# Strassen's scheme for two pairs of feed-forward chunks, and the norm's factors moved from weights to activations

## What is computed

```python
def swiglu(h, w_gate, w_up, w_down):
    return (jax.nn.silu(h @ w_gate) * (h @ w_up)) @ w_down

for l in range(2):
    x = x + 0.5 * swiglu(rms_norm(x, ffn1_norm[l]), ffn1_w_gate[l], ffn1_w_up[l], ffn1_w_down[l])
    ...                                  # attention and pooling, "mix" below
    x = x + 0.5 * swiglu(rms_norm(x, ffn2_norm[l]), ffn2_w_gate[l], ffn2_w_up[l], ffn2_w_down[l])
return rms_norm(x, final_norm)
```

## Time and profile before

| | before |
|---|---|
| median of 3 runs | 936.33 us (936.30 to 936.41) |
| profiled execution | 936.85 us, its span 934.7 us |
| TensorE busy | 925.4 us, 99% |
| VectorE busy | 551.5 us, 59% |
| ScalarE busy | 502.0 us, 54% |
| GpSimd busy | 44.5 us, 5% |
| moved by DMA | 174.67 MB, mean 187 GB/s |

### The profile page before, as it was taken

How to read it: one execution, slowest core, us unless ns; L and a number is a source line. 1 busy time by engine, 2 the same in 40 slices (tenths; PEclk the granted TensorE clock), 3 DMA queues, 4 the chain that set the end, 5 groups by cost and what they waited for, 6 DMA issues and landing times.

```text
span 934.7 us, 12762 instructions
## 1 busy us (share of the span) xinstructions
PE 925.4 (99%) x4313; PEld 759.4 (81%) x4313; DVE 551.5 (59%) x896; ACT 502.0 (54%) x825; POOL 44.5 (5%) x84
## 2 busy tenths in 40 slices
PE   8999999999999999999999999999999999999997
PEld 6788888887778888888888888888877888888886
DVE  5655465559756655556476455564787564554644
ACT  6554454557637545545365455453675464554543
POOL 0010100010001001001010000000100000000000
PEclk9999999999999999999999999999999999999999
DMA  7867778855245677786465657646434276465441
GB/s 245 293 157 209 212 169 235 291 201 185 91 136 178 194 221 198 179 240 168 128 227 197 208 190 250 205 158 214 135 141 147 74 261 206 162 212 192 158 157 45
DMA packets 123676, 174.67 MB, mean 187 GB/s; under 512 B 8400, under 2 KB 99712, under 8 KB 123392
## 3 DMA queue, kind: packets, MB, share of 16 engines
q1 hardware_dynamic: 117744, 165.43, 52.8%
q0 software_dynamic: 2848, 6.38, 5.8%
q10 hardware_dynamic: 3056, 2.49, 0.8%
HBM read 173.14 MB, written 4.19 MB: 190 GB/s over the span
## 4 chain that ended last, share of the span: by engine, by line
PE 96%; DMA 1%; DVE 1%; SPq 1%; ACT 0%; issue 0%; POOLq 0%; POOL 0%
PE ps L1036 29%; PE ps L1039 29%; PE ps L1037 29%; PE ps L1133 2%; DMA w_raw<-in_ffn_w_up_dram 1%; PE ps L1095 1%; PE ps L1046 1%; PE ps L1047 1%; PE ps L1117 1%; PE ps L1271 1%; PE ps L1287 1%; PE ps L1299 1%; PE ps L1315 1%; SPq L313 0%; DVE w_lo L778 0%; PE ps L1259 0%
## 5 line engine op out<-in xcount | busy, mean ns | idle before, releaser
L1036 PE MATMUL ps<-w_hi,xt_hi 128*128 128x512 f32 x848 | 337.5, 398 | 1.1 <-DVE xt_lo L792 0.7
L778 DVE SCALAR_TENSOR_TENSOR w_lo<-w_raw,gains,w_hi 128x512 fp32r<-128x512 f32 x416 | 285.0, 746 | 86.1 <-ACT w_hi L508 82.4
L1037 PE MATMUL ps<-w_lo,xt_hi 128*128 128x512 f32 x848 | 330.5, 390 | 0.0
L1039 PE MATMUL ps<-w_hi,xt_lo 128*128 128x512 f32 x848 | 325.9, 390 | 0.0
L508 ACT ACTIVATE w_hi<-w_raw,gains 128x512 fp32r<-128x512 f32 x408 | 260.8, 714 | 77.6 <-PE ps L1039 76.6
L767 DVE TENSOR_TENSOR w_lo<-w_raw,w_hi 128x1024 fp32r<-128x1024 f32 x104 | 122.7, 1221 | 124.0 <-ACT w_hi L501 123.7
L1036 PEld LDWEIGHTS ps<-w_hi,xt_hi 128*128 128x128 f32 x848 | 159.3, 188 | 36.0 <-issue 2.8
L1039 PEld LDWEIGHTS ps<-w_hi,xt_lo 128*128 128x128 f32 x848 | 159.2, 188 | 34.0
L1037 PEld LDWEIGHTS ps<-w_lo,xt_hi 128*128 128x128 f32 x848 | 159.5, 188 | 30.7
L501 ACT ACTIVATE w_hi<-w_raw 128x1024 fp32r<-128x1024 f32 x104 | 104.4, 1052 | 116.2 <-PE ps L1039 116.2
L1036 PE MATMUL ps<-w_hi,gt_hi 128*128 128x512 f32 (+1 forms) x356 | 138.7, 390 | 0.0
(11 more groups left out here) (95 smaller groups left out, 423.4 us busy)
## 6 DMA issues: line engine op xcount, KB each, us to landing
w_raw<-in_ffn_w_down_dram SPq DMA_DIRECT2D x88, 512.0 KB, 4.3
w_raw<-in_ffn_w_gate_dram SPq DMA_DIRECT2D x86, 512.0 KB, 4.0
w_raw<-in_ffn_w_up_dram SPq DMA_DIRECT2D x86, 512.0 KB, 5.2
w_raw<-in_w_in_dram SPq DMA_DIRECT2D x32, 512.0 KB, 4.9
w_raw<-in_w_out_dram SPq DMA_DIRECT2D x16, 512.0 KB, 5.4
bias_scratch<-in_rpb_dram POOLq DMA_DIRECT2D x32, 96.0 KB, 6.1
bias<-bias_scratch POOLq DMA_DIRECT2D x2, 1536.0 KB, 7.7
resid<-in_x_dram SPq DMA_DIRECT2D x4, 256.0 KB, 5.0
```

Of the source, the lines that this page charges most:

```text
L778: nc.vector.scalar_tensor_tensor(w_lo[slot][:, part], w_raw[slot][:, part], g, w_hi[slot][:, part].bitcast(F32), ALU.mult, ALU.subtract).t ...
L1036: nc.tensor.matmul(o, hi, wh, start=start, stop=False)
L1037: nc.tensor.matmul(o, hi, wl, start=False, stop=False)
L1039: last = nc.tensor.matmul(o, lo, wh, start=False, stop=bool(stop))
```

## The change

**Pairs.** A stage's 11 chunks are now: chunks 0 and 1 as before, then twice a body of four chunks (`ff_body`, index j; i = 4j + 2), then chunk 10. In a body chunks i and i + 3 are ordinary, and chunks i + 1 and i + 2 (3+4 and 7+8) are a pair. Its gate and up product is a 2 x 2 block product: A is the activation (rows: the two tiles, columns: the two halves of the width), B the weights (rows: halves of the width, columns: the two chunks). Seven block products with sums of A's and of B's blocks take the place of eight (the variant of Strassen's scheme with operands A11, A12, A22, S1 to S4), each of 12 matrix instructions (`seventh`). They go into banks 7 (X), 0 (Z) and 1 (Y).

**Sums.** B's four sums are made by VectorE in place in the raw units (`add_units`, 2048 columns), the seven combinations of the results also by VectorE (`combine`, into `normed`'s four quarters `p1`, `m5`, `u`, `c11`), two copies of results out of PSUM by ScalarE. A's sums S1 to S4 are made once a stage.

**Slots.** Two more slots E and F hold units of the pairs. They and the new operands' low parts lie where the mix's `scores`, `z`, `bias`, `pool_m` and `final_gain` lie, so `pool_m` is loaded in each layer and `final_gain` in the last stage.

**Factors.** From chunk 2 on the weights are split without the norm's factors. The activation is multiplied instead: once a stage GpSimd adds `xt_hi` and `xt_lo` into `normed` (two sums of 1024 columns), ScalarE multiplies by the factors in place (eight of 256 columns), ScalarE and VectorE split it into `xs_hi`, `xs_lo`, then GpSimd makes the four sums S in series (512 columns each), and both split these too.

GpSimd, new, between `rstd_of` and the gathers of each feed-forward stage:

```diff
+            def x_sums(layer, ff):
+                number = layer * STAGES + ff["stage"]
+                n = ff_no(layer, ff)
+                pool.wait_ge(xt_lo_ready, number * 4 + 4)
+                for t in range(TT):
+                    nc.gpsimd.tensor_tensor(
+                        normed[:, t, :],
+                        xt_hi[:, t, :, :].rearrange("p k q -> p (k q)").bitcast(F32),
+                        xt_lo[:, t, :, :].rearrange("p k q -> p (k q)").bitcast(F32), ALU.add
+                    ).then_inc(x_summed, 1)
...
+                pool.wait_ge(x_lo_ready, 4 * n + 2)
+                nc.gpsimd.tensor_tensor(block(1, 1), block(1, 1), block(1, 0), ALU.subtract
+                                        ).then_inc(s_summed, 1)
+                pool.wait_ge(s_summed, 4 * n + 1)
+                nc.gpsimd.tensor_tensor(block(1, 0), block(0, 0), block(1, 0), ALU.add
+                                        ).then_inc(s_summed, 1)
...
```

ScalarE, the stage (the first steps) and the body:

```diff
+                split_hi(d, d, raw_no(layer, stage, d, 0), (down_used, down_no(layer, ff, 1)))
+                scale_x(layer, ff)
+                store_gt_hi(layer, ff, 0)
+                x_hi(layer, ff)
+                silu_of(layer, ff, 1, 0)
+                split_hi(a, a, raw_no(layer, stage, a, 2), (g0_used, ord_no(layer, ff, 1) + 1))
+                silu_of(layer, ff, 1, 1)
+                split_hi(b, b, raw_no(layer, stage, b, 2))
+                s_hi(layer, ff)
+                with act.Fori(0, BODIES) as j:
+                    ff_body(layer, ff, j)
...
+                plain(d, d, 3 * j + 1, (down_used, down_no(layer, ff, i)))
+                plain(e, e, 2 * j, (g0_used, ord_no(layer, ff, 2 * j + 1) + 1))
+                store_gt_hi(layer, ff, i - 1)
+                silu_of(layer, ff, 2 * j + 2, 0)
+                sum_hi(f, e, 4 * n + 1, (gu_ready[1], ord_no(layer, ff, 2 * j + 1) + 1))
+                plain(a, a, 2 * j + 3, (g0_used, ord_no(layer, ff, 2 * j + 2) + 1))
+                silu_of(layer, ff, 2 * j + 2, 1)
+                plain(b, b, 3 * j + 3)
+                plain(d, d, 3 * j + 2, (down_used, down_no(layer, ff, i + 1)))
+                copy_m(BANK_X, 7 * n + 1, p1)
+                copy_m(BANK_Z, 7 * n + 2, m5)
+                sum_hi(e, b, 4 * n + 3, (m_ready, 7 * n + 1))
+                store_gt_hi(layer, ff, i)
+                sum_hi(f, f, 4 * n + 2, (m_ready, 7 * n + 2))
...
+                sum_hi(a, a, 4 * n + 4, (m_ready, 7 * n + 3))
...
+                plain(e, e, 2 * j + 1, (m_ready, 7 * n + 5))
...
+                plain(f, f, 2 * j + 1, (m_ready, 7 * n + 6))
...
+                store_gt_hi(layer, ff, i + 1)
+                plain(a, d, 3 * j + 3, (m_ready, 7 * n + 7))
...
```

VectorE, the body (`lo` is the low part of a unit, `gate_pair` a gate with both operands in SBUF; ahead of the loop the list is as ScalarE's, with `x_lo` behind `store_gt_lo(0)` and `s_lo` last):

```diff
+                lo(d, 3 * j + 1, d)
+                lo(e, 3 * j, e)
+                store_gt_lo(layer, ff, i - 1)
+                gate(layer, ff, 2 * j + 2, 0)
...
+                add_units(e, f)
+                lo(f, 3 * j, e)
+                lo(a, 4 * j + 3, a)
+                gate(layer, ff, 2 * j + 2, 1)
+                lo(b, 2 * j + 3, b)
...
+                add_units(f, b)
+                dve.wait_ge(sum_ready, 4 * n + 2)
+                add_units(b, e)
+                lo(d, 3 * j + 2, d)
+                lo(e, 3 * j + 1, b)
+                store_gt_lo(layer, ff, i)
...
+                combine(c11, ps[:, BANK_X, :], p1, ALU.add)
+                lo(f, 3 * j + 1, f)
+                gate_pair(c11, gated, 0, 0, 4 * n + 1)
...
+                add_units(a, b)
+                dve.wait_ge(m_ready, 7 * n + 5)
+                combine(u, ps[:, BANK_Y, :], p1, ALU.add)
...
+                combine(m5, m5, u, ALU.subtract)
...
+                combine(p1, ps[:, BANK_Z, :], m5, ALU.add)
+                lo(a, 4 * j + 4, a)
+                gate_pair(p1, gated_x, 0, 1, 4 * n + 2)
+                dve.wait_ge(m_ready, 7 * n + 6)
+                combine(u, ps[:, BANK_Y, :], u, ALU.add)
+                combine(m5, ps[:, BANK_Y, :], m5, ALU.subtract)
+                lo(e, 3 * j + 2, e)
...
+                combine(u, ps[:, BANK_X, :], u, ALU.subtract)
+                gate_pair(m5, gated_x, 1, 0, 4 * n + 3)
+                lo(f, 3 * j + 2, f)
+                gate_pair(u, gated, 1, 1, 4 * n + 4)
+                store_gt_lo(layer, ff, i + 1)
+                lo(a, 4 * j + 5, d)
+                lo(d, 3 * j + 3, b)
+                store_gt_lo(layer, ff, i + 2)
+                gate(layer, ff, 2 * j + 3, 0)
+                lo(a, 4 * j + 6, a)
+                lo(b, 2 * j + 4, b)
+                gate(layer, ff, 2 * j + 3, 1)
```

TensorE, the body:

```diff
+                ordinary(layer, ff, 2 * j + 2, 0, (a, b), units)
+                transpose_gated(layer, ff, 2 * j + 1)
+                ordinary(layer, ff, 2 * j + 2, 1, (a, b), units)
+                whole_down(layer, ff, i - 1, d, 3 * j + 1)
+                pe.wait_ge(x_lo_ready, 4 * ff_no(layer, ff) + 4)
+                seventh(layer, ff, BANK_X, e, 3 * j, A11)
+                pe.wait_ge(gated_ready[0], ord_no(layer, ff, 2 * j + 2) + 1)
+                seventh(layer, ff, BANK_Z, f, 3 * j, S1)
+                transpose_gated(layer, ff, 2 * j + 2)
+                pe.wait_ge(m_copied, 2 * n + 1)
+                seventh(layer, ff, BANK_X, a, 4 * j + 3, A12)
+                pe.wait_ge(m_copied, 2 * n + 2)
+                seventh(layer, ff, BANK_Z, b, 2 * j + 3, S4)
+                seventh(layer, ff, BANK_Y, e, 3 * j + 1, S2)
+                whole_down(layer, ff, i, d, 3 * j + 2)
+                pe.wait_ge(combined, 7 * n + 2)
+                seventh(layer, ff, BANK_Y, f, 3 * j + 1, S3)
+                pe.wait_ge(combined, 7 * n + 1)
+                seventh(layer, ff, BANK_X, a, 4 * j + 4, A22)
...
+                units = (3 * j + 2, 3 * j + 2)
+                pe.wait_ge(combined, 7 * n + 4)
+                ordinary(layer, ff, 2 * j + 3, 0, (e, f), units, {4: transpose_x})
+                whole_down(layer, ff, i + 1, a, 4 * j + 5)
+                pe.wait_ge(pair_gated, 4 * n + 4)
+                transpose_tiles(gated)
+                pe.wait_ge(combined, 7 * n + 6)
+                ordinary(layer, ff, 2 * j + 3, 1, (e, f), units)
+                whole_down(layer, ff, i + 2, d, 3 * j + 3)
```

SyncE loads in the order in which the units are used, from the body's E on only once the stage's first gate and up product is done. In the body it waits before each load until the raw unit's last reader is done; the end of a body goes as follows:

```diff
+                    free(d, 3 * j + 3)
+                    load_down(layer, weights, i + 1, d)
+                    sp.wait_ge(sum_ready, 4 * pair_no(layer, ff, j) + 4)
+                    load_down(layer, weights, i + 2, b)
+                    free(a, 4 * j + 5)
+                    load_gate_up(layer, weights, i + 4, 0, a)
+                    free(d, 3 * j + 4)
+                    load_gate_up(layer, weights, i + 4, 1, b)
```

467 lines of the change are left out of this document (336 added, 131 removed).

## The result

| | before | after |
|---|---|---|
| median of 4 runs each, same chip | 936.37 us | 950.84 us (950.47 to 952.86) |
| ratio, with its interval | 1 | 1.016 [1.0148, 1.0172] |
| span of the profiled execution | 934.7 us | 948.7 us |

The kernel became 1.6% slower. The forecast was 938.3 us, the range ended at 950.0, so the result lies outside it. The page after, to be held against the earlier trace rows: the span, the busy times, TensorE's granted clock in 40 slices, the chain by engine.

What follows compares the result with a forecast made beforehand. TensorE was taken as the bound, busy 925.4 of 934.7 us. From 936.85, minus 21.8 for products, plus 3 x 5.75 + 6.55 = 23.8 of waits, gave 938.85; the runs' median being 0.5 lower, 938.3 us, range 924 to 950.

Steps and rivals of the forecast that it cites:

- Products: TensorE's gate and up products: 84 in place of 96 per two chunks, 0.227 us each, 21.8 us less.
- The steady body: Four-chunk body with VectorE starting on time: TensorE needs 64.5 us and stalls 0.85 us a body.
- about 0.5 us at F and 0.3 at the a unit: TensorE's expected waits for w_lo in each body, for f's first half and for the a unit, eight times.
- VectorE late in every body: Slower rival: longer VectorE waits use up the 0.5 us slack in each of eight bodies; 945 to 955 us, chance 0.18.
- The start of a stage: GpSimd's new sums, in turns with w_lo, delay each stage's first body; 5.75 us lost a stage, 6.55 in the first.
- turn: GpSimd's new sums and VectorE's w_lo, both with two SBUF operands, alternate: 1.08 us a sum, 1.2 a w_lo half.
- L: VectorE's lateness in a stage's first body: 12.0 us after body start where 7.7 is steady, 4.3 us; first stage 3.1.
- +0.3: Predicted lengthening in us of each stage but the first: 5.45 us of products gained, 5.75 lost.
- The estimate of 1.2 and 2.3 us: GpSimd's sums of 512 and 1024 columns by the Trainium skill; would make the forecast sum about 941 us.
- At nothing: Items priced at zero, SP's new waits among them: units free 7 to 9 us early, transfers landing in 5.2.
- The rival with this mechanism: Transfers set the pace: five units asked for within some 10 us, about 5 us in each second body; 958 us, chance 0.06.

Runs made afterwards that it cites:

- c4: c3 with the two wide sums of 1024 columns also on VectorE, ahead of the first gate, so GpSimd makes no sum; 936.07 us.
- e1: Kernel after, with the 16 gathers of layer 1's attention bias moved from layer 0's second feed-forward stage to layer 0's mix; 948.74 us.
- e2: Kernel after, with the second body's E and F units asked for as soon as their slots are free; 940.48 us.
- e5: Kernel after without GpSimd's four serial sums S1 to S4, blocks of A standing in for them; 937.35 us.
- c3: Kernel after with three alterations: E and F asked for early, sums S on VectorE, order behind S3 altered; 933.50 us, again 934.54 us.

## Why the prediction was wrong, and where it was right

**Products: right.** 96 fewer, 0.227 us apart in the new blocks, at full clock.

**The steady body: right in place, with the terms swapped about.** The forecast had about 0.5 us at F and 0.3 at the a unit; the waits view has eight of 0.3 and eight of 0.2, the body 65.64 for 65.35. "VectorE late in every body", the rival of the slower side, did not happen.

**The start of a stage: right, with two sums mis-sized that nearly cancel, which is luck.** GpSimd's 512 columns take 1.30 us and not 1.08, 1024 take 2.37 and not 1.9 (1.9 times the 0.69 and 1.22 of VectorE, where 1.5 to 1.6 was taken over from small operations); with a turn they take 2.16 where 1.08 + 1.2 was laid down. VectorE begins the sum e+f at 330.89, 11.6 us behind the body's first product (319.27), where 12.0 was said: L is 3.9, not 4.3. All in all layer 1, second stage: +0.55 for +0.3. The Trainium skill, "SBUF — State Buffer", section "Who interferes with whom", calls the lock exclusive between the two engines; the trace before agrees for one direction, this one for both (w_lo 2.36 to 4.39, and in c4 GpSimd's 0.55 to 1.42). The estimate of 1.2 and 2.3 us from the Trainium skill, "GPSIMD Engine Reference", section 3.1, was nearer than my terms from the rows of this case.

**What failed first: "At nothing", SP's new waits.** I took transfers of 5.2 us from the earlier trace rows and set 7 to 9 us of free time against them. The free time was there, 10.3 us for the down unit's second half. The transfer was what I had wrong: in the burst that half took 8.0 us in layer 1, without gathers, and 16.6 and 14.3 beside them in layer 0.

The rival with this mechanism was named, at 0.06, and dismissed with the argument that 0.74 busy at 196 GB/s makes 265 when full, 4 us a unit, so that each is in time. The rate held beside gathers: 234 GB/s at 0.89 and 247 at 0.96 are 263 and 257 when full, where layer 1, without gathers, has 262 at 0.75, which is 349. The stretch of the earlier trace rows had gathers in it too; in the kernel before, from 60 to 90 us, four of them already took 19.7% of the engines' time. What did not follow is that each unit is in time. These loads did not land in the order in which they were asked for: a half of F asked for at 100.16 landed after 13.1 us, at 113.3, ahead of the down unit's half, asked for at 99.62 and there at 116.2. The rival in turn was priced in the second bodies of all four stages; it came true in layer 0's alone. e1 and e2 price it: 3.4 us in the second stage, once the fall of the clock in the first body is taken off the 4.45, and 5.3 in the first, its fall of the clock among it.

**What failed second: waits were priced at their own length.** No term held a fall of TensorE's clock. Behind waits of 2 us it cost 1.0 us more each time that it came (1.01, 1.04 and 1.07, in three stages with and without). The kernel after has two of these, in layer 0's second stage and in layer 1's first; behind the 3.17 us wait the stretch from 119 to 131 lost 0.28 x 12 = 3.4 us of clock. What fell in layer 0 is inside its excess, not on top of it.

Together: of 12 us of excess, 9.75 is what e1 and e2 took away in layer 0 (8.7 by transfers, with the falls behind them, and 1.07 a fall behind the first body's own wait), 1.0 the fall in layer 1's first stage, and 1.0 the quarter of a microsecond by which each of the four stages was forecast too short.

**The balance of the change.** With loads in time and the clock up a stage gains 5.45 us of products and is 0.55 longer: 6.0 us of cost, 3.05 of it the serial sums S (e5), the rest, by subtraction and not by a run, the steady bodies' waits and the wide sums with their turns. In c3, 2 to 3 us of the 21.8 are left over.

## What to carry to other kernels

Before a change asks the DMA queues for several units at once, look at what else runs in that stretch, gathers of small pieces above all: a transfer time taken from a steady trace says nothing of a burst, and the late engine that a wait names may be two releases away from the load that is late. A rate when full, divided by the number of units, does not give the time at which a unit in a burst lands. Work put on GpSimd to relieve VectorE is not free where both read two operands from SBUF, in either direction; price it as turns, and look for the small steps on the path too. When a change makes the bound engine wait for 2 us where it never waited, its clock can fall, so add about 1 us to such a wait and expect runs that differ from each other.
